# A third seven-product group per feed-forward chunk, weight sums made by adding DMAs, and banks handed on in two steps

## The chip, the cores and the metric

The kernel runs on one core of one Trainium2 chip. The metric is the device time of one execution, in microseconds. The kernel before took 2149.78 us, the median of three runs (2149.24 to 2150.08).

## The reference, cut to what matters

Two layers of a streaming encoder on 256 tokens with a model width of 2048, in float32. Layer 0 mixes tokens by sliding-window attention, layer 1 by a gated linear recurrence; both also attend into 256 memory tokens. Each layer ends in a feed-forward block of width 5632, and that block is all the change touches:

```python
        x = x + jnp.concatenate([mix, mem_out], axis=-1) @ w_o[i]
        gate, up = _split(rms_norm(x, norm_ffn[i]) @ w_gate_up[i], (D_FF, D_FF))
        x = x + (jax.nn.silu(gate) * up) @ w_down[i]
```

`w_gate_up` is 2048 by 11264 and `w_down` 5632 by 2048, for each of the two layers.

## The kernel before, in words

**Products in two parts.** TensorE works on float32r. Every weight block arrives by DMA in `raw`. ScalarE writes its rounded high part to `w_hi` (L644) and VectorE the remainder to `w_lo` (L1104), in the place of `raw`. The activations have a high and a low part too (`hT` for the normalised input, `gT` for the feed-forward's middle). A product is three matmuls of 128x128 by 128x512: high by high, low by high, high by low.

**Pieces and rings.** A piece is 256 rows by 512 columns of a weight (512 KB), two blocks of 128 rows. SyncE loads the pieces in the order in which they are used, into `raw`, a ring of eight. `w_hi` is a ring of four, so ScalarE can round piece n only once TensorE has used piece n-4 (`piece_used`). `pieces()` in the streams of ScalarE and VectorE is the frame of their order: step i first does the work written for step i, and then the split of piece i+3. Each engine runs its stream in order, so everything written for a step delays the splits behind it.

**The chunk loop.** The 5632 columns of gate and of up are cut into eleven chunks of 512. The first is computed plainly, the other ten in a loop of five passes over two halves, which are called passes here when counted one by one. One such pass has 16 pieces: for each of eight quads (256 rows of the weight) a piece of gate and a piece of up. A plain quad takes 24 matmuls (two row blocks, gate and up, two tiles of tokens, three parts). In two quads of a pass (`SEVEN = (2, 5)`) a Strassen-like scheme takes seven products in place of eight, so 21 matmuls. It needs three sums of the four weight blocks: `seven_sums` (VectorE, L1123, L1126, L1128) makes them one piece ahead of the group's split, `sums_high` (ScalarE) and `sums_low` (VectorE, L1134, L1135) split them. It also needs combinations of the activations, made once per layer (`seven_forms`).

**Banks.** Four PSUM banks belong to a pass (`own`), and the other four (`shared`) take the products that a seven-product group gives to several results. The next pass has these roles swapped. So the shared banks must be read out (`shared_products`, VectorE L1600 to L1605, with one copy by ScalarE) before the next pass begins, which `own_free` tells TensorE; the own banks are read right after the pass's last piece (`own_products`, L1613 to L1615).

**The product.** During pass n the result of pass n-1 is finished: tanh (ScalarE, step 2), `gate_silu` and `times_up` (VectorE, steps 4 and 5), a transpose in 32x32 squares to `turned`, sixteen DMAs of 32 KB that complete the transpose (SyncE's queue, put between the pieces 13, 14 and 15), and `moved_block` (VectorE L1209, step 12), which writes the low part of `gT`.

**Down.** After the loop `down_products` multiplies `gT` by `w_down`, with five seven-product groups of its own on each side. Before it starts, TensorE waits for `own_free` and for the twenty blocks of `gT` that the loop wrote.

## Time and profile before

| what | value |
|---|---|
| median of three runs | 2149.78 us |
| profiled execution, its own time | 2150.24 us |
| its span, first to last instruction | 2148.5 us |
| TensorE busy | 2135.4 us, 99% of the span |
| VectorE busy | 1682.8 us, 78% |
| ScalarE busy | 1119.4 us, 52% |
| GpSimd busy | 56.6 us, 3% |
| DMA: moved, mean rate | 435.56 MB, 203 GB/s |
| TensorE clock granted | 1.00 |

The busy time of an engine is a mean over stages that differ. The chain of waits is followed back from the last instruction, each step to what released it. In a timeline the instructions of an engine stand in order of time, with the idle time ahead of one in square brackets and the engine that ended it; like instructions that follow one another are one line with a count, and what is shown for them is the start of the first and the time to the end of the last. Two instructions of one engine overlap a little, so what a step costs is read from one start to the next.

### The profile page before, as it was taken

The page shows a single profiled execution, that of the slowest core. Times are in us where ns is not written, and L with a number is a line of the kernel's source. Part 1 is how long each engine was busy: PE and PEld are TensorE (multiplying, and loading weights), DVE is VectorE, ACT ScalarE, POOL GpSimd, SP SyncE. Part 2 cuts the span into 40 slices and gives each one's busy share as a digit, 9 for nine tenths or more (in the row PEclk, how much of TensorE's full clock was granted, in tenths as well). Part 3 has the DMA queues.
Part 4 walks back from the last instruction along what each step waited for, and adds up shares of the span by engine and source line. Part 5 has one row for each costly group of instructions (what it writes and reads, how often), then busy time and mean ns, then how long its engine had stood idle before and what let it go on. Part 6 is the DMA issues. An engine that isn't in the chain of part 4 may idle for free.

```text
span 2148.5 us, 29147 instructions
## 1 busy us (share of the span) xinstructions
PE 2135.4 (99%) x9992; PEld 1777.8 (83%) x9992; DVE 1682.8 (78%) x2139; ACT 1119.4 (52%) x1478; POOL 56.6 (3%) x99
## 2 busy tenths in 40 slices
PE   8999999999999999999999999999999999999999
PEld 7888888888888888888888888888888888888887
DVE  6657766898988898777666767667989898898775
ACT  7755654555455555454544544455554555555453
POOL 2101100000000000000000000000000000000000
PEclk9999999999999999999999999999999999999999
DMA  9765467667666766675665656577676667666664
GB/s 327 243 197 147 132 211 207 206 203 227 209 205 201 232 207 211 191 226 180 212 175 158 197 159 199 163 222 205 203 224 210 200 209 227 208 210 202 227 199 138
DMA packets 244568, 435.56 MB, mean 203 GB/s; under 512 B 23040, under 2 KB 43648, under 8 KB 244480
## 3 DMA queue, kind: packets, MB, share of 16 engines
q1 hardware_dynamic: 243392, 432.31, 65.1%
q10 hardware_dynamic: 1088, 2.10, 0.3%
q8 instruction: 52, 0.85, 0.2%
q14 instruction: 36, 0.29, 0.0%
HBM read 411.25 MB, written 2.10 MB: 192 GB/s over the span
## 4 chain that ended last, share of the span: by engine, by line
PE 99%; ACT 0%; DVE 0%; DMA 0%; issue 0%; DVEq 0%; SPq 0%; ACTq 0%
PE unit_bank L1886 30%; PE mix_bank L1928 24%; PE unit_bank L1928 24%; PE mix_bank L1898 7%; PE unit_bank L1898 7%; PE mix_bank L1886 4%; PE mix_bank L1979 1%; PE mix_bank L2109 1%; PE mix_bank L2044 0%; PE mix_bank L2006 0%; PE mix_bank L2053 0%; PE mix_bank L2095 0%; DVE w_lo L1104 0%; PE mix_bank L2017 0%; PE mix_bank L2028 0%; DMA source_T<-in_mem_T 0%
## 5 line engine op out<-in xcount | busy, mean ns | idle before, releaser
L644 ACT ACTIVATE w_hi<-raw 128x1024 fp32r<-128x1024 f32 x767 | 798.1, 1057 | 828.2 <-DVE sum_all L1128 166.5
L1104 DVE TENSOR_TENSOR w_lo<-raw,w_hi 128x1024 fp32r<-128x1024 f32 x767 | 923.4, 1221 | 353.0 <-ACT w_hi L644 346.8
L1886 PE MATMUL unit_bank<-w_hi,hT_hi 128*128 128x512 f32 (+1 forms) x576 | 181.2, 396 | 0.0
L1886 PE MATMUL unit_bank<-w_hi,hT_lo 128*128 128x512 f32 (+1 forms) x576 | 176.2, 387 | 0.0
L1886 PE MATMUL unit_bank<-w_lo,hT_hi 128*128 128x512 f32 (+1 forms) x576 | 175.9, 387 | 0.0
L1928 PE MATMUL unit_bank<-w_lo,hT_hi 128*128 128x512 f32 x480 | 147.9, 389 | 0.0
L1928 PE MATMUL mix_bank<-w_lo,hT_hi 128*128 128x512 f32 x480 | 147.8, 389 | 0.0
L1928 PE MATMUL mix_bank<-w_hi,hT_hi 128*128 128x512 f32 x480 | 147.8, 389 | 0.0
L1928 PE MATMUL unit_bank<-w_hi,hT_hi 128*128 128x512 f32 x480 | 147.8, 389 | 0.0
L1928 PE MATMUL unit_bank<-w_hi,hT_lo 128*128 128x512 f32 x480 | 147.8, 389 | 0.0
L1928 PE MATMUL mix_bank<-w_hi,hT_lo 128*128 128x512 f32 x480 | 147.7, 389 | 0.0
L1886 PEld LDWEIGHTS unit_bank<-w_hi,hT_lo 128*128 128x128 f32 x576 | 107.9, 188 | 21.7
L1886 PEld LDWEIGHTS unit_bank<-w_lo,hT_hi 128*128 128x128 f32 x576 | 107.9, 188 | 21.7
L1886 PEld LDWEIGHTS unit_bank<-w_hi,hT_hi 128*128 128x128 f32 x576 | 104.5, 188 | 18.2 <-DVE w_lo L1104 0.2
L1928 PEld LDWEIGHTS mix_bank<-w_hi,hT_hi 128*128 128x128 f32 x480 | 90.1, 188 | 18.7
L1928 PEld LDWEIGHTS unit_bank<-w_hi,hT_hi 128*128 128x128 f32 x480 | 90.1, 188 | 18.7
L1928 PEld LDWEIGHTS unit_bank<-w_lo,hT_hi 128*128 128x128 f32 x480 | 90.1, 188 | 18.7
L1928 PEld LDWEIGHTS mix_bank<-w_lo,hT_hi 128*128 128x128 f32 x480 | 90.1, 188 | 18.7
L1928 PEld LDWEIGHTS unit_bank<-w_hi,hT_lo 128*128 128x128 f32 x480 | 90.1, 188 | 18.7
L1928 PEld LDWEIGHTS mix_bank<-w_hi,hT_lo 128*128 128x128 f32 x480 | 90.1, 188 | 18.7
L1928 PE MATMUL mix_bank<-w_hi,gT_lo 128*128 128x512 f32 x272 | 83.8, 389 | 0.0
L1928 PE MATMUL unit_bank<-w_hi,gT_lo 128*128 128x512 f32 x272 | 83.8, 389 | 0.0
(427 smaller groups left out, 3602.7 us busy)
## 6 DMA issues: line engine op xcount, KB each, us to landing
raw<-in_w_gate_up SPq DMA_DIRECT2D x352, 512.0 KB, 4.4
raw<-in_w_down SPq DMA_DIRECT2D x176, 512.0 KB, 4.6
raw<-in_w_in_b SPq DMA_DIRECT2D x104, 512.0 KB, 3.7
raw<-in_w_o SPq DMA_DIRECT2D x64, 512.0 KB, 3.8
raw<-in_w_in_a SPq DMA_DIRECT2D x40, 512.0 KB, 3.7
moved<-turned SPq DMA_DIRECT2D x528, 32.0 KB, 2.5
raw<-in_w_mem_kv SPq DMA_DIRECT2D x31, 512.0 KB, 5.5
tanh_ff<-act_ff SPq DMA_DIRECT2D x112, 32.0 KB, 3.0
```

Source lines behind the costliest of these rows:

```text
L644: act.activation(w_hi[:, s, :, :], raw[:, r, :, :], ACT.Copy).then_inc(sems["hi_ready"], 1)
L1104: dve.tensor_tensor(w_lo[:, r, :, :], raw[:, r, :, :], w_hi[:, s, :, :].bitcast(F32), ALU.subtract).then_inc(sems["lo_ready"], 1)
L1886: ins = pe.matmul(all_banks[2 * pair + tile][:, 0:cols], stationary[part][:, kt + j, tile * P:(tile + 1) * P], b[:, j, 0:cols], start=open ...
L1898: ins = pe.matmul(bank[:, :], x_parts[part], w, start=start and m == 0, stop=stop and m == 2)
L1928: ins = pe.matmul(own[2 * tile + side][:, :], x[part][:, kt + j, tile * P:(tile + 1) * P], w, start=opens and j == 0 and m == 0, stop=clos ...
L1979: ins = pe.transpose(mix_bank[b][:, n * P:(n + 1) * P], src[:, n * width:(n + 1) * width], ident[:, :])
L2109: ins = pe.matmul(mix_bank[b][:, h * P:(h + 1) * P], early_key[:, h, :], whole(query_in, h * P + half, (4 * P - half, TILES), (size, block ...
```

## The change

What it does:

- **Groups.** `SEVEN` goes from (2, 5) to (2, 4, 6): three of the eight quads of a pass are seven-product groups. `QUAD_KTS` sets which weight rows a quad takes, so that the groups take rows at 4, 8 and 10 (before 4 and 10). The activations' combinations for the third come from `late_form` and `late_form_lo`, once per layer.
- **Sums.** Two of the three weight sums of a group are no longer computed by VectorE. SyncE loads the upper gate block twice, into both halves of a sum buffer (`spread`), and GpSimd's queue then issues two DMAs that add the lower gate block and the upper up block to it (`chunk_weight_sums`, `accum_op=ALU.add`). The gate piece of such a quad loads only its lower block. There are three such buffers; two of them lie where `kmT_b` and `vm_b` (layer 1's memory keys and values) lie, which are therefore written to the output's DRAM when layer 0's output projection begins, and read back during its down products. VectorE makes the other two sums (`third_sum`, `fourth_sum`), for which it now waits as late as the group's own split.
- **Banks.** The last group now ends at step 14 and not 12, so `shared_products` moves to step 14 (before 13) and `moved_block` to step 15 (before 12). The banks that the next pass's gate pieces write are released first (`own_free`), those of its up pieces second (`own_late`).
- **Silu** and its product with up move one step earlier (3 and 4); the transpose is now at step 6.
- **GpSimd.** The masks for the recurrence are made between the layers, since the third group's forms lie in their place.

```diff
-SEVEN = (2, 5)
-SEVEN_APART = 6
+SEVEN = (2, 4, 6)
+SEVEN_APART = 4
+QUAD_KTS = (0, 2, 4, 6, 8, 12, 10, 14)
+SPREAD_STEPS = (0, 1, 5)
+LAST_SEVEN = 2 * SEVEN[-1] + 2
...
+            def spread(w, kt, col, b, used):
+
+                sp.wait_ge(sems["piece_used"], t.value("piece_used", used))
+                for m in range(2):
+                    sp.dma_start(chunk_sums[b].two[:, m, :], w[kt * P:(kt + 1) * P, bass.ds(col, COLS)]).then_inc(sems[f"spread{b}"], 16)
...
+                spread_after = [2 * q + 2 - CHUNK_PIECES for q in SEVEN]
...
                     for half in range(2):
+                        col = j * (2 * COLS) + (1 + half) * COLS
                         for n in range(CHUNK_PIECES):
-                            piece(wg, n // 2 * 2, j * (2 * COLS) + (1 + half) * COLS + n % 2 * D_FF)
+                            load = lower_half_piece if n in SEVEN_PIECES else piece
+                            load(wg, QUAD_KTS[n // 2], col + n % 2 * D_FF)
+                            if n in SPREAD_STEPS:
+                                m = SPREAD_STEPS.index(n)
+                                spread(wg, QUAD_KTS[SEVEN[m]], col, chunk_sum(half, m), n + 1 - spread_after[m])
                             chunk_turns(n)
...
+            def chunk_weight_sums(layer):
...
+                            pool.wait_ge(sems[f"spread{b}"], t.next(f"spread{b}", 32))
+                            pool.dma_start(chunk_sums[b].two[:, 0, :], w[(kt + 1) * P:(kt + 2) * P, bass.ds(col, COLS)],
+                                           accum_op=ALU.add).then_inc(sems[f"summed{b}"], 16)
+                            pool.dma_start(chunk_sums[b].two[:, 1, :], w[kt * P:(kt + 1) * P, bass.ds(col + D_FF, COLS)],
+                                           accum_op=ALU.add).then_inc(sems[f"summed{b}"], 16)
...
+            def third_sum(sums, b):
+
+                r = slot[0] % RAW
+                blocks = four_blocks(raw, r)
+                dve.wait_ge(sems[f"summed{b}"], t.next(f"summed{b}", 32))
+                dve.wait_ge(sems[f"arrived{r}"], t.value(f"arrived{r}", -16))
+                dve.tensor_tensor(blocks[:, 0, :], sums.two[:, 1, :], blocks[:, 1, :], ALU.add).then_inc(sems["sum_ready"], 1)
+
+            def fourth_sum(sums, used):
...
+                dve.wait_ge(sems["piece_used"], t.value("at", used))
+                dve.wait_ge(sems[f"arrived{r + 1}"], t.value(f"arrived{r + 1}", -16))
+                dve.wait_ge(sems["sum_ready"], t.next("sum_ready"))
+                dve.tensor_tensor(sums.all[:, :], blocks[:, 0, :], blocks[:, 3, :], ALU.add).then_inc(sems["sum_ready"], 1)
+                dve.wait_ge(sems["sum_ready"], t.next("sum_ready"))
...
                 def shared_products(shared):
 
                     dve.wait_ge(sems["first_copied"], t.next("first_copied"))
-                    dve.wait_ge(sems["piece_used"], t.value("at", 1))
+                    dve.wait_ge(sems["piece_used"], t.value("at"))
                     dve.tensor_tensor(act_ff[:, 1, :], shared[3][:, :], up_ff[:, 0, :], ALU.subtract).then_inc(sems["dve_chain"], 1)
                     dve.wait_ge(sems["dve_chain"], t.next("dve_chain"))
-                    dve.tensor_tensor(act_ff[:, 0, :], shared[1][:, :], act_ff[:, 1, :], ALU.add)
-                    dve.tensor_tensor(up_ff[:, 1, :], shared[2][:, :], act_ff[:, 1, :], ALU.add).then_inc(sems["dve_chain"], 1)
+                    dve.tensor_tensor(up_ff[:, 1, :], shared[2][:, :], act_ff[:, 1, :], ALU.add).then_inc(sems["own_free"], 1)
+                    t.move("own_free")
+                    dve.tensor_tensor(act_ff[:, 0, :], shared[1][:, :], act_ff[:, 1, :], ALU.add).then_inc(sems["dve_chain"], 1)
...
-                def chunk(j, own, shared):
+                def chunk(j, half, own, shared):
 
                     for i in pieces(CHUNK_PIECES):
-                        if i + LEAD + 1 in SEVEN_PIECES:
-                            seven_sums(chunk_sums)
+                        if i + LEAD in SEVEN_PIECES:
+                            n = SEVEN_PIECES.index(i + LEAD)
+                            b = chunk_sum(half, n)
+                            third_sum(chunk_sums[b], b)
+                            fourth_sum(chunk_sums[b], i - (2 * SEVEN[n - 1] + 2) if n else 0)
                         if i + LEAD - 2 in SEVEN_PIECES:
-                            sums_low(chunk_sums)
+                            sums_low(chunk_sums[chunk_sum(half, SEVEN_PIECES.index(i + LEAD - 2))])
+                        if i == 3:
+                            gate_silu()
                         if i == 4:
-                            gate_silu()
-                        if i == 5:
                             times_up()
-                        if i == 12:
+                        if i == 6:
+                            turn_product()
+                        if i == LAST_SEVEN:
+                            shared_products(shared)
+                        if i == LAST_SEVEN + 1:
                             moved_block(gT, j * 4, "gT_ready")
-                        if i == 13:
-                            shared_products(shared)
                     own_products(own)
```

VectorE's stream around the end of a pass. `w_lo` is the split of a piece, `act_ff` and `up_ff` read the banks (shared ones first, the pass's own after), `gT_lo` is `moved_block`. Before:

```order
L1104 TENSOR_TENSOR w_lo<-raw,w_hi 128x1024 [waits hi_ready]
...
L1209 TENSOR_TENSOR gT_lo<-moved,gT_hi 128x4x4x32
...
L1104 TENSOR_TENSOR w_lo<-raw,w_hi 128x1024 [waits hi_ready]
L1600 TENSOR_TENSOR act_ff<-mix_bank,up_ff 128x512 [waits piece_used,first_copied]
...
L1602 TENSOR_TENSOR act_ff<-mix_bank,act_ff 128x512 [waits dve_chain]
L1603 TENSOR_TENSOR up_ff<-mix_bank,act_ff 128x512
...
L1605 TENSOR_TENSOR act_ff<-mix_bank,up_ff 128x512 [waits dve_chain]
...
L1104 TENSOR_TENSOR w_lo<-raw,w_hi 128x1024 [waits hi_ready]
...
L1613 TENSOR_TENSOR act_ff<-unit_bank,act_ff 128x512 [waits own_free]
```

The same place in the changed kernel:

```order
L1172 TENSOR_TENSOR w_lo<-raw,w_hi 128x1024 [waits hi_ready]
L1688 TENSOR_TENSOR act_ff<-mix_bank,up_ff 128x512 [waits piece_used,first_copied]
...
L1690 TENSOR_TENSOR up_ff<-mix_bank,act_ff 128x512 [waits dve_chain]
L1692 TENSOR_TENSOR act_ff<-mix_bank,act_ff 128x512
...
L1695 TENSOR_TENSOR act_ff<-mix_bank,up_ff 128x512 [waits dve_chain]
...
L1172 TENSOR_TENSOR w_lo<-raw,w_hi 128x1024 [waits hi_ready]
...
L1295 TENSOR_TENSOR gT_lo<-moved,gT_hi 128x4x4x32
...
L1172 TENSOR_TENSOR w_lo<-raw,w_hi 128x1024 [waits hi_ready]
L1703 TENSOR_TENSOR act_ff<-unit_bank,act_ff 128x512 [waits own_late,piece_used]
```

The shared banks' four sums stand one step nearer to the end (three splits lay between them and the own banks' sums, now two), and the two `gT_lo` have moved from ahead of them to behind them.

VectorE's stream between the first and the second group of a pass, from silu on. `raw<-` is a sum that is written back to the ring, `turned` the transpose. Before:

```order
L1581 SCALAR_TENSOR_TENSOR tanh_ff<-tanh_ff,act_ff 128x512 [waits tanh_ff_ready]
...
L1104 TENSOR_TENSOR w_lo<-raw,w_hi 128x1024 [waits hi_ready]
...
L1589 SCALAR_TENSOR_TENSOR up_ff<-up_ff,half_rs_87,tanh_ff 128x512 [waits shared_free]
...
L1185 STREAM_TRANSPOSE turned<-up_ff 128x4x4x32 [waits dve_chain]
...
L1104 TENSOR_TENSOR w_lo<-raw,w_hi 128x1024 [waits hi_ready]
...
L1123 TENSOR_TENSOR sums<-raw 128x1024 [waits arrived3,arrived2]
```

And in the changed kernel:

```order
L1667 SCALAR_TENSOR_TENSOR tanh_ff<-tanh_ff,act_ff 128x512 [waits tanh_ff_ready]
...
L1172 TENSOR_TENSOR w_lo<-raw,w_hi 128x1024 [waits hi_ready]
...
L1675 SCALAR_TENSOR_TENSOR up_ff<-up_ff,half_rs_94,tanh_ff 128x512 [waits shared_free]
...
L1172 TENSOR_TENSOR w_lo<-raw,w_hi 128x1024 [waits hi_ready]
L1204 REGISTER_ALU [waits summed1]
L1205 TENSOR_TENSOR raw<-key_sums_69,raw 128x512 [waits arrived0]
L1213 REGISTER_ALU [waits arrived1,piece_used]
L1214 TENSOR_TENSOR sum_all<-raw 128x512 [waits sum_ready]
...
L1172 TENSOR_TENSOR w_lo<-raw,w_hi 128x1024 [waits hi_ready]
...
L1271 STREAM_TRANSPOSE turned<-up_ff 128x4x4x32 [waits dve_chain]
```

The second group begins two pieces earlier in the pass than before, so its two sums and its splits now stand in the stretch that holds silu, the product with up and the transpose.

## Rows read from the trace of the kernel before

**Rows 1.** The page, part 4: shares of the chain that ended last.
```profile
PE 99%; ACT 0%; DVE 0%; DMA 0%; issue 0%; DVEq 0%; SPq 0%; ACTq 0%
```

**Rows 2.** Windows: window, busy us by engine (instructions), granted clock, DMA share, GB/s.
```profile
372.19:793.79 421.60, 421.60 (x1861) 349.12 (x1861) 373.87 (x420) 218.43 (x250) 0.00 (x0) 1.00 0.68 211
16.00:24.00 8.00, 8.00 (x37) 6.61 (x36) 6.84 (x12) 5.81 (x11) 0.00 (x0) 1.00 1.05 408
```

**Rows 3.** Timeline, TensorE: start us, us, line, what, count; two starts in one pass.
```profile
467.23 0.39 PE L1898 MATMUL unit_bank<-w_hi,hT_hi 128*128 128x512 f32 x1
...
487.63 0.62 PE L1928 MATMUL unit_bank<-w_hi,hT_hi 128*128 128x512 f32 x2
```

**Rows 4.** Timeline, VectorE, first half of that pass; idle time before in brackets.
```profile
456.63 1.29 DVE L1613 TENSOR_TENSOR act_ff<-mix_bank,act_ff 128x512 f32<-128x512 f32 x2
...
459.04 1.21 DVE L1123 TENSOR_TENSOR sums<-raw 128x1024 f32<-128x1024 f32 x1
460.29 0.69 DVE L1126 TENSOR_TENSOR raw<-sums,raw 128x512 f32<-128x512 f32 x1
461.01 0.69 DVE L1128 TENSOR_TENSOR sum_all<-raw 128x512 f32<-128x512 f32 x1
...
465.09 1.23 DVE L1104 TENSOR_TENSOR w_lo<-raw,w_hi 128x1024 fp32r<-128x1024 f32 x1 [0.95 <-ACT w_hi L644]
466.55 1.23 DVE L1134 TENSOR_TENSOR sums_lo<-sums,sums_hi 128x1024 fp32r<-128x1024 f32 x1 [0.24 <-ACT sums_hi L658]
...
468.30 1.22 DVE L1104 TENSOR_TENSOR w_lo<-raw,w_hi 128x1024 fp32r<-128x1024 f32 x1
469.43 1.28 DVE L1581 SCALAR_TENSOR_TENSOR tanh_ff<-tanh_ff,act_ff 128x512 f32<-128x512 f32 x2
470.63 1.22 DVE L1104 TENSOR_TENSOR w_lo<-raw,w_hi 128x1024 fp32r<-128x1024 f32 x1
471.77 1.41 DVE L1589 SCALAR_TENSOR_TENSOR up_ff<-up_ff,half_rs,tanh_ff 128x512 f32<-128x512 f32 x2
473.21 1.30 DVE L1185 STREAM_TRANSPOSE turned<-up_ff 128x512 f32<-128x512 f32 x2
474.44 1.18 DVE L1104 TENSOR_TENSOR w_lo<-raw,w_hi 128x1024 fp32r<-128x1024 f32 x1
```

**Rows 5.** Timeline, VectorE, end of the same pass.
```profile
488.92 1.23 DVE L1104 TENSOR_TENSOR w_lo<-raw,w_hi 128x1024 fp32r<-128x1024 f32 x1 [2.99 <-ACT w_hi L644]
490.06 1.29 DVE L1209 TENSOR_TENSOR gT_lo<-moved,gT_hi 128x512 f32 x2
491.39 1.23 DVE L1104 TENSOR_TENSOR w_lo<-raw,w_hi 128x1024 fp32r<-128x1024 f32 x1
492.53 0.69 DVE L1600 TENSOR_TENSOR act_ff<-mix_bank,up_ff 128x512 f32<-128x512 f32 x1
...
495.19 3.49 DVE L1104 TENSOR_TENSOR w_lo<-raw,w_hi 128x1024 fp32r<-128x1024 f32 x3
```

**Rows 6.** Timeline, ScalarE, same pass.
```profile
461.82 1.06 ACT L644 ACTIVATE w_hi<-raw 128x1024 fp32r<-128x1024 f32 x1 [4.21 <-DVE sum_all L1128]
462.78 1.32 ACT L939 ACTIVATE tanh_ff<-act_ff,half_rs 128x512 f32<-128x512 f32 x2
```

**Rows 7.** Timeline, SyncE's queue, same pass.
```profile
474.55 3.69 SPq L432 DMA_DIRECT2D moved<-turned  x6
...
485.96 15.97 SPq L417 DMA_DIRECT2D raw<-in_w_gate_up  x9
```

**Rows 8.** DMA issues: transfer, count, KB each, median us to landing.
```profile
raw<-in_w_gate_up SPq DMA_DIRECT2D x352, 512.0 KB, 4.4
...
x_tok<-in_mem SPq DMA_DIRECT2D x4, 512.0 KB, 10.9
...
raw<-in_w_mem_kv SPq DMA_DIRECT2D x2, 256.0 KB, 3.8
```

More of the change, by code:

```diff
@@ L278, in trunk @@
         assert rest + 2 * 2 * 3 * P * 4 <= nc.sbuf_usable_end
-        chunk_sums = Sums(sums, sums_lo, sum_all, sum_all_lo, sums_hi)
+        chunk_sums = tuple(Sums(two, two_lo, sum_all, sum_all_lo, sums_hi)
+                           for two, two_lo in ((sums, sums_lo), key_sums[0], key_sums[1]))
+        chunk_forms = [tuple(f[:, g, :, :] for f in forms) for g in range(2)]
+        chunk_forms.append(tuple(f[:, :, :] for f in late_forms))
         over = arena + 2 * FT * SEQ * 4
@@ L498, in projection_ffn @@
                 wo = w_o[layer, :, :]
+                if layer == 0:
+                    for n, tile in enumerate((kmT_b, vm_b)):
+                        sp.dma_start(aside(n), tile[:, :, :].rearrange("p a n -> p (a n)")).then_inc(sems["parked"], 16)
                 for kts in MIXED_KTS:
@@ L526, in projection_ffn @@
                         moves(down_turns[p])(n)
+                        if layer == 0 and p == 0 and n == 10:
+                            for m, tile in enumerate((kmT_b, vm_b)):
+                                sp.dma_start(tile[:, :, :].rearrange("p a n -> p (a n)"), aside(m)).then_inc(sems["restored"], 16)
             wa = w_in_a[0, :, :]
@@ L968, in projection_ffn @@
                     for half, (own, shared) in enumerate(chunk_banks):
-                        chunk(j * 2 + half, shared)
+                        chunk(j * 2 + half, half, shared)
                 def store(c):
@@ L1677, in projection_ffn @@
                     for half, (own, shared) in enumerate(chunk_banks):
-                        chunk(j * 2 + half, own, shared)
+                        chunk(j * 2 + half, half, own, shared)
                 def down_form(n):
@@ L1899, in product, with seven_products @@
                 return ins
-            def seven_products(x, kt, forms, n, sums, own, shared, first, last, shared_ready):
+            def seven_products(x, kt, forms, sums, own, shared, first, last, shared_ready):
                 s, r = slot[0] % RING, slot[0] % RAW
@@ L1945, in down_products @@
                         pe.wait_ge(sems["gT_ready"], t.next("gT_ready", TILES))
+                    if p == 0 and (q, side) == (0, 1):
+                        pe.wait_ge(sems["own_late"], t.next("own_late"))
                     if q not in DOWN_SEVEN:
@@ L1960, in chunk_products @@
                         n = SEVEN.index(q)
-                        seven_products(hT, 2 * q, forms, n, chunk_sums, own, shared, n == 0, n == len(SEVEN) - 1, evicted)
+                        seven_products(hT, QUAD_KTS[q], chunk_forms[n], chunk_sums[chunk_sum(half, n)], own, shared, n == 0, n == len(SEVEN) - 1, evicted)
                         continue
                     for side in range(2):
-                        plain_piece(hT, 2 * q, side, own, q == 0, q == CHUNK_PIECES // 2 - 1)
+                        if q == 0 and side == 1:
+                            pe.wait_ge(sems["own_late"], t.next("own_late"))
+                        plain_piece(hT, QUAD_KTS[q], side, own, q == 0, q == CHUNK_PIECES // 2 - 1)
             def unit(stationary, pair, kts=ALL_KTS, opens=True, closes=True, cols=COLS):
```

146 lines of the change are left out of this document (105 added, 41 removed).

## The prediction

> **What bounds the kernel now.** I read the page's chain first: TensorE makes up 99% of it [rows 1]. Then the windows, cut to the ten passes of layer 0's chunk loop: they take 421.60 us and TensorE is busy in all of it, at a granted clock of 1.00 [rows 2]. So a pass takes 42.16 us. By the code it holds six plain quads and two groups, 6 x 24 + 2 x 21 = 186 matmuls; 42.16 / 186 = 0.2267 us for one, 2.72 us for a plain piece (12) and 4.76 us for a group (21). No pass waits for anything. What matters next is how near the other engines are to being late, since a matmul taken away brings everybody's deadline nearer. VectorE is busy for 373.87 of the 421.60 us [rows 2], 37.4 us a pass; DMA engines 0.68 of the time at 211 GB/s. Last I followed one pass in the timelines, to see where VectorE stands when a group begins. The first group of the pass begins at 467.23 [rows 3] and needs the split of its second piece, which starts on VectorE at 465.09 [rows 4] and takes 1.23 us: ready at 466.32, 0.91 us early. That is all the slack there is. Later in the pass VectorE waits for TensorE (2.99 us idle ahead of 488.92) [rows 5].
>
> **The matmuls removed.** One more group in each of 20 passes: 20 x 3 x 0.2267 = 13.6 us less, a pass of 183 matmuls or 41.48 us.
>
> **VectorE, in sum.** The two wide sums of a pass go (459.04, 1.21 us each); the third group adds two sums of 0.69 us and its low parts, 1.75 us (466.55 to 468.30) [rows 4]. That is 37.4 - 2.4 + 3.1 = 38.1 us in 41.48, 92%. It fits in the mean, so the mean doesn't decide; the order does.
>
> **VectorE, from the last group to the next pass's first.** The order in which its work now stands is this. Count from T, the moment TensorE goes on after the pass's last group; in the trace of before the like moment (after its second group) is 487.63 [rows 3]. Splits go no further ahead, because `w_hi` has four places: the third-next split can start only when the group has ended. ScalarE's and VectorE's first split follow, VectorE's at 488.92, so T + 1.29 [rows 5]. From there, start to start:
>
> - the split of the next pass's piece 0, 1.14 us (488.92 to 490.06) [rows 5]: T + 2.43
> - four sums from the shared banks, 2.66 us (492.53 to 495.19) [rows 5]: T + 5.09
> - split of piece 1: T + 6.23
> - two `gT_lo`; their 1.33 us (490.06 to 491.39) [rows 5] hold a short wait, and two instructions of that size take 1.20 (469.43 to 470.63) [rows 4], so 1.20: T + 7.43
> - split of piece 2: T + 8.57
> - four sums from the own banks, 2.41 us (456.63 to 459.04) [rows 4]: T + 10.98
> - split of piece 3: T + 12.12, where `third_sum` starts; it ends 0.69 later, T + 12.81
> - ScalarE had waited for this sum; then it rounds piece 4, makes the two tanh, and rounds piece 5. In before, the same chain leads from the end of the last sum (461.01 + 0.69 = 461.70) by ScalarE at 461.82 and 462.78 [rows 6] to VectorE's split at 465.09 [rows 4]: 3.39 us. So the split starts at T + 16.20 and ends at T + 17.43.
>
> TensorE has six plain pieces for that time, 6 x 2.72 = 16.32 us. It waits 1.11 us at the first group. In before the shared sums and `gT_lo` lie before the end of the pass, and VectorE begins the own sums 0.3 us after it (456.63, for a pass that starts four plain pieces ahead of 467.23, at 456.35) [rows 3, 4].
>
> **VectorE, on to the second group.** It has no pause in which to catch up: low parts start 1.46 us after that split (465.09 to 466.55) and take 1.75, silu 1.20, a split 1.14, the product with up 1.33 (471.77 to 473.21 is 1.44 with the wait ahead of the transpose), a split 1.14 [rows 4]: T + 24.22. Then the third sum (0.69 and 0.03 of semaphore, as 460.29 to 461.01 shows) and the fourth, 0.72 each. ScalarE rounds piece 8 once the third sum is there: 0.12 to start (461.70 to 461.82) and 1.06 [rows 6], so VectorE's split starts at T + 26.11, the transposes take 1.23 (473.21 to 474.44) and the split of piece 9 ends at T + 29.70. TensorE: group started at T + 17.43, 4.76, two plain pieces 5.44: T + 27.63. It waits 2.07 us. Before, this stretch held no second group: it comes two pieces later there. For the third group the count goes on: low parts 1.75, two splits 2.28, two sums 1.4 (the fourth also waits for the second group's end, T + 34.46), two splits 2.3: T + 37.7 for a need at T + 39.90, no wait.
>
> A pass then takes 41.48 + 1.11 + 2.07 = 44.66 us, 2.50 more than before, with VectorE idle at its end again; so the lag doesn't grow from pass to pass. Of the ten passes of a layer the first has no shared sums and no `gT_lo` ahead of it: its first group is ready at 9.1 us for a need at 10.88, its second 0.33 us late.
>
> **Into the down products.** TensorE waits there for all twenty blocks of `gT`. The last two are now written at T + 6.23 to T + 7.5, and TensorE gets there at T + 5.44: 2.1 us, each layer. Before they were written some 8 us ahead (490.06 for a pass that ends at 498.5) [rows 5].
>
> **The sum.** 18 passes x (1.11 + 2.07) = 57.2; two first passes x 0.33 = 0.7; two down starts 4.2; less 13.6: +48.5 us. On the profiled execution's 2150.24 us (span 2148.5 and 1.7 around it) that makes 2198.7; the median of the runs is 0.5 lower, so 2198.3.
>
> **The adding DMAs.** No row shows one. Bytes: 12 transfers of 0.26 MB a pass come and three halves of pieces go, +2.4 MB; 211 GB/s x 42.16 us is 8.9 MB, so 11.3 MB in 44.66 us, 252 GB/s, or 287 if an add counts its bytes twice, since it reads its target too. An early window moves 408 GB/s for 8 us [rows 2]. Only if the six adds (1.6 MB) held the engines for over five times their bytes would the rings be full. Time: SyncE is held by `turned`, now ready at T - 16.1 (the transposes end at T + 28.5 and the next T comes 44.66 later, with 0.1 for the wait); its sixteen small DMAs with the loads between take 11.4 us (474.55 to 485.96) [rows 7], so the next pass's piece 0 is issued at T - 4.6 and its first spread about T - 4.2. The sum is wanted at T + 12.1: 16.3 us for a spread and an add. At 3.8 us each, as the 256 KB loads [rows 8], that is 7.6; at 10.9 each, as the 512 KB loads of the crowded start [rows 8], it is 21.8, 5.5 us late in each pass, some +105 us. I take the first, it is nearer in size; both ends go into the range. Piece 0 itself has 4.8 us for a landing of 4.4 in the median [rows 8]; each us that it is late costs one in a pass, 18 in all. Less than nothing it can't cost: what VectorE saves by it is already out of the list. The Trainium skill (DMA: Bandwidth & Descriptors, "Where 436 GB/s comes from") gives about 358 GB/s as the limit of HBM for a core; the trace's 408 is above it, and at 358 the 12.8 MB would still take 36 us of 44.66, hidden.
>
> GpSimd issues the adds with nothing else to do: it is not busy at all in this window [rows 2]. The Trainium skill (SBUF — State Buffer, "Who interferes with whom") says that descriptor generation on GpSimd starves while VectorE runs in a two-port mode, but that tensor_tensor has none; by that the adds are not held, and no run here shows it.
>
> **At nothing:** the forms (once a layer, under the plain chunk), the masks (GpSimd is free between the layers), moving 1 MB aside and back (waited for a whole stage later). Together at most a few us.
>
> **The rivals.**
> - *The lag is absorbed*, the other side of no change: 13.6 us less, and the 4.2 at the down starts at most: 2136 to 2140. It needs 3.2 us less on VectorE between T and the second group. For it speaks the mean (38.1 of 41.48); against it, every term is a row of this same loop and the slack of 0.91 us in before leaves no room.
> - *The waits are half of what I count*, 0.7 us a pass: 18 x 0.7 + 5 - 13.6 = +4 us, within or near no change, 2150 to 2160.
> - *The DMAs decide*: adds or piece 0 late by 1 to 5.5 us a pass, 2216 to 2300. For it: a burst of eight transfers that start within 4 us after SyncE was held; against it: 408 GB/s in the early window.
>
> **How the numbers follow.** Forecast 0.68, with its own range 2182 to 2215 (0.5 us a pass to either side, and a few more for DMAs). Absorbed 0.07, halved waits 0.07, DMAs 0.18, of which half stays under 2250. The range 2176 to 2250 leaves out about 0.2. A measurement of this kernel can't tell less than 0.2% (4.3 us) from no change. Faster 0.08, same 0.04, slower 0.88.
>
> **What would show it.** Right: passes of about 44.7 us; TensorE idle about 1.1 us ahead of a pass's first group and 2.1 ahead of the second, ended by VectorE's `w_lo`, none ahead of the third; 2 us at each down start, ended by `gT_lo`; VectorE without a pause from the last group on to the second. Wrong: passes of 41.5 us; waits ended by a DMA into `raw` or by the sum's semaphore; VectorE idle before `third_sum`; instructions of VectorE longer than in before beside the adds.

## The result, and the profile after

| kernel | median of its runs | range | runs | ratio to before, 95% interval |
|---|---|---|---|---|
| before | 2149.88 us | 2149.24 to 2150.08 | 4 | |
| changed | 2216.63 us | 2215.01 to 2219.17 | 4 | 1.0312, 1.0294 to 1.0330 |

The change costs 66.8 us where I forecast 48.5. The direction and the place were right, the size was 18 us short. (The kernel before has one run more here than in the table ahead of the prediction.)

The profiled execution took 2217.19 us, its span is 2214.9, and its mean granted clock 0.994 (before 1.000). The chain of the page, which was TensorE for 99% [rows 1]:

```profile
PE 73%; DVE 8%; DMA 7%; issue 5%; ACT 4%; SPq 2%; DVEq 0%; ACTq 0%
```

It now runs over VectorE, SyncE's queue and transfers too: TensorE waits. The list of its waits says for whom (line, what it waited for, us in all, times, longest):

```profile
PE mix_bank L2023 <- DVE w_lo L1172: 27.6, 20, 1.8
PE unit_bank L2023 <- DVE w_lo L1172: 22.4, 16, 1.8
...
PE unit_bank L2053 <- issue: 4.1, 2, 2.1
```

That is 36 waits at the start of a seven-product group (L2023): two in each of the 18 passes that are not the first of a layer. They end with VectorE's split. The last line is the start of the down products, once per layer. The windows answer to [rows 2]: the ten passes of layer 0, and one typical pass.

```profile
372.80:825.60 452.80, 425.46 (x1831) 345.21 (x1830) 377.93 (x440) 233.56 (x271) 48.98 (x56) 0.99 0.81 246
517.89:562.74 44.85, 42.12 (x184) 34.20 (x184) 37.88 (x44) 23.24 (x28) 5.25 (x6) 1.00 0.81 246
```

VectorE's work per pass hardly grew (37.8 against 37.4 us); the pass grew from 42.16 to 44.85. Where the time goes, TensorE's timeline of that pass shows at the starts of its three groups and of the next pass's first:

```profile
517.89 0.50 PE L2023 MATMUL mix_bank<-w_hi,hT_hi 128*128 128x512 f32 x1 [0.95 <-DVE w_lo L1172]
...
530.19 0.50 PE L2023 MATMUL mix_bank<-w_hi,hT_hi 128*128 128x512 f32 x1 [1.78 <-DVE w_lo L1172]
...
540.54 0.39 PE L2023 MATMUL mix_bank<-w_hi,hT_hi 128*128 128x512 f32 x1
...
562.74 0.50 PE L2023 MATMUL unit_bank<-w_hi,hT_hi 128*128 128x512 f32 x1 [0.95 <-DVE w_lo L1172]
```

The third group comes 10.35 us after the second, which is one group and two plain pieces (10.20) and 0.15: no wait, as forecast. From the first to the second it is 12.30, against the same 10.20: 2.1 us lost. From the third to the next pass's first it is 22.20, where one group and six plain pieces take 21.08: 1.1 us lost. The idle time in brackets is some 0.16 us smaller than the wait, since the end of a matmul's row overlaps the next. The first matmul after a wait stands as 0.50 instead of 0.39 us, and the next starts 0.34 us later instead of 0.227.

VectorE after the same moment T = 545.31 (the third group's start and its 4.77), to be held against [rows 4, 5]:

```profile
546.60 1.23 DVE L1172 TENSOR_TENSOR w_lo<-raw,w_hi 128x1024 fp32r<-128x1024 f32 x1 [2.88 <-ACT w_hi L705]
547.74 0.68 DVE L1688 TENSOR_TENSOR act_ff<-unit_bank,up_ff 128x512 f32<-128x512 f32 x1
...
553.86 1.28 DVE L1703 TENSOR_TENSOR act_ff<-mix_bank,act_ff 128x512 f32<-128x512 f32 x2
...
557.39 0.68 DVE L1205 TENSOR_TENSOR raw<-sums,raw 128x512 f32<-128x512 f32 x1
558.84 0.69 DVE L1214 TENSOR_TENSOR sum_all<-raw 128x512 f32<-128x512 f32 x1 [0.77 <-DMA raw<-in_w_gate_up]
559.66 1.23 DVE L1172 TENSOR_TENSOR w_lo<-raw,w_hi 128x1024 fp32r<-128x1024 f32 x1
561.46 1.23 DVE L1172 TENSOR_TENSOR w_lo<-raw,w_hi 128x1024 fp32r<-128x1024 f32 x1 [0.57 <-ACT w_hi L705]
...
572.57 1.30 DVE L1271 STREAM_TRANSPOSE turned<-up_ff 128x512 f32<-128x512 f32 x2
573.79 1.18 DVE L1172 TENSOR_TENSOR w_lo<-raw,w_hi 128x1024 fp32r<-128x1024 f32 x1
```

Reading it from T: the first split at T + 1.29 (forecast 1.29), own sums at 8.55 (8.57), third sum at 12.08 (12.12), the split that the first group needs at 16.15 (16.20), the one that the second needs ends at 574.97, T + 29.66 (29.70). The count from rows of before holds to 0.05 us over thirty instructions. One thing in it was not forecast: the fourth sum waits 0.77 us for the load of piece 5, which was issued late (T + 1.0) and landed 12.3 us after its issue. In this pass it costs nothing, since ScalarE's chain ends at the same time: VectorE's next split but one still waits 0.57 us for ScalarE.

**The part that was missing: the clock.** In some passes the matmuls after the second wait run slower. TensorE's timeline of one such pass, and the windows of that stretch and of the one behind it (the last three figures are granted clock, DMA share, GB/s):

```profile
438.93 0.50 PE L2023 MATMUL mix_bank<-w_hi,hT_hi 128*128 128x512 f32 x1 [1.78 <-DVE w_lo L1172]
...
440.43 0.62 PE L2023 MATMUL unit_bank<-w_hi,hT_hi 128*128 128x512 f32 x1
440.84 0.63 PE L2023 MATMUL unit_bank<-w_hi,hT_lo 128*128 128x512 f32 x1
...
443.83 0.40 PE L2023 MATMUL unit_bank<-key_sums_lo,forms_hi 128*128 128x512 f32 x1
```

```profile
440.43:443.83 3.40, 3.40 (x9) 2.64 (x8) 3.06 (x4) 0.00 (x0) 0.00 (x0) 0.50 0.31 71
443.83:447.00 3.17, 3.17 (x15) 2.64 (x14) 0.81 (x2) 1.37 (x2) 0.00 (x0) 1.00 0.54 185
```

From 440.43 to 443.83 eight matmuls start 0.42 to 0.43 us apart instead of 0.227, at a granted clock of 0.50 (the level of 1.2 GHz), 1.5 us after the wait is over, and then it is 1.00 again. The loss is 8 x 0.2 = 1.6 us. The Trainium skill (TensorE: Matmul & The Clock Gate, "Wait — 56ns, not 53.3ns?") gives 426.7 ns between such matmuls at the lower clock; the trace agrees with 426 to 427 inside such a stretch. This happens in 6 of the 18 passes with waits (from 440.4, 621.3, 757.9 and from 1590.7, 1727.2, 1908.2) and at both down starts. The down start of layer 0:

```profile
825.57 0.71 PE L2053 MATMUL unit_bank<-w_hi,gT_hi 128*128 128x512 f32 x2 [2.01 <-issue]
826.11 1.03 PE L2053 MATMUL unit_bank<-w_hi,gT_lo 128*128 128x512 f32 x2
826.94 1.05 PE L2053 MATMUL unit_bank<-w_lo,gT_hi 128*128 128x512 f32 x2
```

Pairs come 0.83 to 0.85 us apart instead of 0.453. The releaser of that wait is not named, but VectorE's `gT_lo` ends at 825.47 (824.18, 1.29 us for its two), 0.10 us before.

**The account**, from starts of the profiled executions: the loop of layer 0 with its down start went from 421.6 to 452.9 us, that of layer 1 from 421.6 to 452.6, each down phase takes 1.7 more, the start of the kernel 0.6: 31.3 + 31.0 + 3.4 + 0.6 = 66.3, which is what the span grew by (66.4; another 0.6 of the execution lies outside the span). In my terms:

| term | forecast | measured |
|---|---|---|
| 60 matmuls less | -13.6 | -13.6 |
| 18 passes with two waits, each | 3.18, in all 57.2 | 44.85 - 41.48 = 3.37, in all 60.7 |
| first passes | 0.7 | about 1.0 |
| waits at the two down starts (start to start) | 4.2 | 2.17 + 2.23 = 4.4 |
| slower matmuls at the lowered clock | 0 | 6 x 1.6 + 2 x 1.7 = 13.0 |
| the kernel's start, one longer wait (1.39 instead of 0.95) | 0 | 1.0 |
| sum | +48.5 | +66.5 |

(The 1.7 at a down start holds 0.1 for starting again. The longer wait is the one at 744.13: the fourth sum ahead of it waited 0.91 us for its piece, so in that pass a transfer did cost TensorE 0.4 us.)

**The queues.** SyncE's and GpSimd's timelines around T:

```profile
540.88 0.38 SPq L431 DMA_DIRECT2D raw<-in_w_gate_up  x1
541.51 0.82 SPq L448 DMA_DIRECT2D sums<-in_w_gate_up  x2
```

```profile
547.01 0.87 POOL L637 DMA_DIRECT2D sums<-in_w_gate_up  x1 [27.90 <-DMA sums<-in_w_gate_up]
547.74 1.02 POOL L639 DMA_DIRECT2D sums<-in_w_gate_up  x1
...
557.02 0.87 POOL L639 DMA_DIRECT2D key_sums<-in_w_gate_up  x1 [6.17 <-issue]
```

Piece 0 is issued at T - 4.4 (forecast T - 4.6) and the first spread at T - 3.8. The spread takes 5.5 us (541.51 to the first add at 547.01), and both adds are issued by T + 3.5, for a need at T + 12.1. Between the rows shown stands a third add, at 549.97; the fourth is issued only after 6.17 us for which the profile names no releaser; it still is in time. The landings say more: the second add landed at 556.66, 0.35 us before the fourth was issued. All 39 such pauses of over 0.4 us in the changed kernel's trace (those with no releaser named) end 0.25 to 0.35 us after the landing of the add two places before. Landings got slower everywhere in the loop, a piece from 4.4 us [rows 8] to 6.5 in the median:

```profile
raw<-in_w_gate_up SPq DMA_DIRECT2D x292, 512.0 KB, 6.5
...
key_sums<-in_w_gate_up SPq DMA_DIRECT2D x80, 256.0 KB, 6.6
key_sums<-in_w_gate_up POOLq DMA_DIRECT2D x80, 256.0 KB, 6.8
```

### The profile page after: what moved, and what is told of

It is laid out like the page before. It is cut to its first block, busy times and chain, and to the rows that moved or that the text cites. A ratio compares the mean times of both kernels' runs of the same rounds, so it can differ in the third digit from the quotient of the medians.

```text
span 2214.9 us, 30087 instructions
## 1 busy us (share of the span) xinstructions
PE 2146.5 (97%) x9932; PEld 1772.1 (80%) x9932; DVE 1697.4 (77%) x2193; ACT 1149.8 (52%) x1522; POOL 162.8 (7%) x220
## 4 chain that ended last, share of the span: by engine, by line
PE 73%; DVE 8%; DMA 7%; issue 5%; ACT 4%; SPq 2%; DVEq 0%; ACTq 0%
PE unit_bank L2011 29%; PE mix_bank L2053 12%; PE unit_bank L2053 12%; DMA raw<-in_w_gate_up 7%; PE unit_bank L2023 6%; PE mix_bank L2023 6%; PE mix_bank L2011 4%; DVE w_lo L1172 3%; ACT w_hi L705 2%; SPq L462 1%; DVE turned L1271 1%; PE mix_bank L2108 1%; PE mix_bank L2238 1%; DVE raw L1205 1%; DVE tanh_ff L1667 1%
## 5 line engine op out<-in xcount | busy, mean ns | idle before, releaser
L2011 PEld LDWEIGHTS unit_bank<-w_lo,hT_hi 128*128 128x128 f32 x576 | 107.9, 188 | 21.7
L2011 PEld LDWEIGHTS unit_bank<-w_hi,hT_lo 128*128 128x128 f32 x576 | 107.9, 188 | 21.7
L2053 PE MATMUL mix_bank<-w_hi,hT_hi 128*128 128x512 f32 x400 | 123.1, 389 | 0.0
L2053 PE MATMUL unit_bank<-w_hi,hT_lo 128*128 128x512 f32 x400 | 123.1, 389 | 0.0
L2053 PE MATMUL unit_bank<-w_hi,hT_hi 128*128 128x512 f32 x400 | 123.1, 389 | 0.0
L2053 PE MATMUL mix_bank<-w_hi,hT_lo 128*128 128x512 f32 x400 | 123.1, 389 | 0.0
L2053 PE MATMUL mix_bank<-w_lo,hT_hi 128*128 128x512 f32 x400 | 123.1, 389 | 0.0
L2053 PE MATMUL unit_bank<-w_lo,hT_hi 128*128 128x512 f32 x400 | 123.1, 389 | 0.0
L2011 PEld LDWEIGHTS unit_bank<-w_hi,hT_hi 128*128 128x128 f32 x576 | 104.4, 188 | 18.2 <-DVE w_lo L1172 0.2
L2053 PE MATMUL unit_bank<-w_hi,gT_hi 128*128 128x512 f32 x272 | 84.8, 394 | 4.1 <-issue 4.1
L2053 PEld LDWEIGHTS unit_bank<-w_lo,hT_hi 128*128 128x128 f32 x400 | 75.1, 188 | 15.6
L2053 PEld LDWEIGHTS unit_bank<-w_hi,hT_hi 128*128 128x128 f32 x400 | 75.1, 188 | 15.6
L2053 PEld LDWEIGHTS unit_bank<-w_hi,hT_lo 128*128 128x128 f32 x400 | 75.1, 188 | 15.6
```

The costliest lines, as they stand in the source:

```text
L2011: ins = pe.matmul(all_banks[2 * pair + tile][:, 0:cols], stationary[part][:, kt + j, tile * P:(tile + 1) * P], b[:, j, 0:cols], start=open ...
L2053: ins = pe.matmul(own[2 * tile + side][:, :], x[part][:, kt + j, tile * P:(tile + 1) * P], w, start=opens and j == 0 and m == 0, stop=clos ...
```

## The experiments

Theory 1: VectorE's work in order, from the last group of a pass to the second of the next, decides; 13 of the 67 us are the lowered clock behind the waits that it makes. Rivals: the transfers decide and VectorE only shows it; VectorE has room and something else is slow. Each run is compared with runs of the kernel before on the same chip. Two further variants with less work for VectorE (`gT_lo` on a quarter of its columns, alone and with the lighter silu and a later tanh) have no result.

### Loads in place of adds

```diff
-pool.dma_start(chunk_sums[b].two[:, 0, :], w[(kt + 1) * P:(kt + 2) * P, bass.ds(col, COLS)], accum_op=ALU.add)
+pool.dma_start(chunk_sums[b].two[:, 0, :], w[(kt + 1) * P:(kt + 2) * P, bass.ds(col, COLS)])
```

(and the second add likewise)

> The 120 adding DMAs become plain loads of the same bytes into the same buffers from the same queue, so the weight sums are not sums; all else stands. Theory (VectorE's work between a pass's last group and the next pass's second group is 3.2 us longer than TensorE's): no change from 2216.6, 2211 to 2218 (at most the 0.8 us that the fourth sum waits for a piece goes, which is covered by ScalarE). Rival 1 (adding in flight is slow and holds the rings): at least 10 us faster, 2150 to 2205.

Measured: 2216.64 us (2215.14 to 2218.47), ratio 1.0309 (1.0292 to 1.0326), TensorE's waits as in the changed kernel (the other banks' line is 22.0 us in 16):

```profile
PE mix_bank L2021 <- DVE w_lo L1170: 28.5, 20, 1.8
```

So that a transfer adds costs nothing here. It does show in the queue: in this run four such transfers are issued from 544.74 to 549.46, with no pause but the wait for the second spread, where the adds stopped after three.

### Two groups, with all the rest of the change

```diff
-SEVEN = (2, 4, 6)
+SEVEN = (2, 5)
...
-SPREAD_STEPS = (0, 1, 5)
+SPREAD_STEPS = (0, 3)
```

> One part alone: two groups as before the change, at quads 2 and 5, with the rest of the change (sums by adding DMAs, two sums by VectorE at the group's own step, banks in two steps, silu a step earlier). VectorE does 2.4 us less in a pass than before and the second group lies later. Theory: no wait, the same 186 matmuls, so the time before: 2150 (2147 to 2153). Rival 1 or 2 (the new DMAs cost by themselves): 2156 or more.

Measured: 2150.08 us (2149.51 to 2151.04), ratio 1.0002 (0.9992 to 1.0011), no wait in any pass. The window of layer 0's loop, to compare with [rows 2]:

```profile
372.50:794.00 421.50, 421.50 (x1862) 349.00 (x1861) 350.28 (x401) 219.05 (x251) 31.59 (x36) 1.00 0.80 246
```

VectorE is 23.6 us less busy than before and the time is the same: TensorE has the whole of it either way. With two groups the adding DMAs (two thirds of their number), the handover and the parked key buffers cost nothing; the whole loss comes with the third group and what it does to the order.

### Tanh and silu one step later

```diff
-if i == 2:
+if i == 3:
     gate_tanh()      # ScalarE
...
-if i == 3:
+if i == 4:
     gate_silu()      # VectorE
-if i == 4:
+if i == 5:
     times_up()
```

> Only order: ScalarE's two tanh one step later (3, before 2), VectorE's silu and its product with up one step later (4 and 5). The tanh no longer lie between ScalarE's splits of the first group's two pieces, behind which VectorE stood idle, and the fourth sum's idle time goes too. Theory: first wait 1.1 to about 0.2 us, second 2.0 to about 1.4, some 27 us in 18 passes, and the lowered clock after the longer waits comes more rarely: 2185 (2178 to 2194). Rivals 1 and 2: within 5 us of 2216.6.

Measured: 2189.39 us (2186.05 to 2191.83), ratio 1.0181 (1.0164 to 1.0198). ScalarE's two tanh leave the chain that leads to the first group. The first wait is gone or under 0.9 us, the second is 1.2 to 1.7 us still, once 2.5:

```profile
PE mix_bank L2023 <- DVE w_lo L1172: 18.3, 13, 2.5
PE unit_bank L2023 <- DVE w_lo L1172: 15.1, 16, 1.7
```

27 us less for one line on each of two engines. A transfer-bound loop would not have moved.

### The product's low part before the last group's end

```diff
-if i == LAST_SEVEN + 1:
+if i == LAST_SEVEN - 1:
     moved_block(gT, j * 4, "gT_ready")
```

(on both engines; two small buffers change places so that nothing is overwritten too early)

> Against the changed kernel: gT's block is written at step 13 (before 15), while VectorE waits for the third group's end; for that the sums' high parts and the forms change places in memory. 1.2 us leave VectorE's stretch, and the down products find gT ready. Theory: the stretch is shorter by 1.2, but the fourth sum then waits for its piece, which lands 13.4 us after the third group's end in the changed kernel's trace, so the first wait falls by 0.8 (1.1 to 0.3), the second stays; at each down start 2.1 of wait and 1.9 of lowered clock go: 18 x 0.8 + 2 x 4 = 22, so 2195 (2188 to 2204). Rival 2 (the DMAs' bytes set the pace): only the down starts' 8 us, 2208 or more.

Measured: 2195.74 us (2194.55 to 2197.97), ratio 1.0214 (1.0198 to 1.0229). No wait at the down starts, and the group waits fall by 6.5 us in sum:

```profile
PE mix_bank L2022 <- DVE w_lo L1171: 23.5, 18, 1.8
PE unit_bank L2022 <- DVE w_lo L1171: 20.0, 14, 1.9
```

The second wait is 1.80 us still, as in the changed kernel, but only three passes have slower matmuls after it instead of six. The gain of 20.9 us is the down starts with their slower matmuls (4.4 + 3.4), 6.5 of waits, three stretches at the lower clock (4.8) and some restarts. So the expected time came true, but not by its terms: 14.4 us were expected from the waits, and no fewer slow stretches in the passes. VectorE's 1.2 us less bring the first wait down by 0.4 us in the mean and not by 0.8, since loads come late behind them. In a pass of layer 0, for example, ScalarE waits 1.42, 1.85 and 2.28 us for loads into `raw` (680.73, 683.64 and 686.98), VectorE's split at 684.73 waits 0.88 for ScalarE, and the fourth sum at 691.02 waits 0.93 for its piece. The loads are a second limit, close behind VectorE's order.

### Silu and its product with up on 64 of 512 columns

```diff
-gate_silu()
+small_silu()     # tanh_ff[:, s, 0:64]
-times_up()
+small_up()       # up_ff[:, s, 0:64]
```

> The changed kernel with silu and its product with up in the ten passes of a layer's loop computed on 64 of 512 columns; the rest of those columns is left out, so the two instructions of each pair shrink from 0.6 us to some 0.1 us. Nothing else is touched. Theory 1 (VectorE's order sets the waits, and the lowered clock after them is part of their price): about 2 us of VectorE's work go between a pass's first and second group, so the wait of 1.95 us ahead of the second group goes (18 x 1.95 = 35 us), and with it the six stretches of slower matmuls in the passes (6 x 1.6 = 9.6 us): 2216.6 - 45 = 2172, range 2166 to 2178. The wait of 1.1 us ahead of the first group and that of 2 us at each down start stay as they are. Theory 2 (the transfers set the pace, VectorE only shows it): 2205 or more, with the second wait still there and ended by a transfer. Theory 3 (the lowered clock has to do with something other than the waits): the waits go and the clock cost stays, 2181.

Measured: 2172.32 us (2170.75 to 2175.01), ratio 1.0107 (1.0090 to 1.0124). The first wait and the down starts stay (0.95 each in the trace), the second is gone, and none of the passes has slower matmuls; the one stretch of them that is left in the trace is at a down start. The other down start has none behind a wait as long as in the changed kernel (2.01).

```profile
PE mix_bank L2040 <- DVE w_lo L1173: 9.5, 10, 1.0
PE unit_bank L2040 <- DVE w_lo L1173: 8.3, 8, 1.3
...
PE unit_bank L2070 <- issue: 4.5, 2, 2.5
```

Its gain over the changed kernel is 44.3 us; 18 x 1.95 for the waits and 9.5 for the clock make 44.6. So the slow stretches in the passes go with the second waits; waits of 0.95 have none behind them. Transfers were the same in number and size, even at 259 GB/s instead of 246, so they did not set the loop's time.

### One handover of the shared banks

```diff
 pe.wait_ge(sems["own_free"], t.next("own_free"))
+pe.wait_ge(sems["own_late"], t.next("own_late"))
 for q in range(CHUNK_PIECES // 2):
...
-        if q == 0 and side == 1:
-            pe.wait_ge(sems["own_late"], t.next("own_late"))
```

> The changed kernel, but TensorE waits at the start of a pass for both releases of the shared banks at once, as the kernel before did, and not in two steps. Theory 1: no difference, 2216.6 within 3 us: the fourth shared sum ends about 5.1 us after the last group by my count and TensorE begins the next pass at 5.44, so even the later release is there in time. Theory 2 (the two steps save a wait that the trace hides): the next pass starts some tenths of a us late in each of 18 passes, 2220 to 2230.

Measured: 2216.31 us (2214.11 to 2216.74), ratio 1.0304 (1.0287 to 1.0321). No difference. In the changed kernel's trace the fourth shared sum ends at 550.47, T + 5.16, and the next pass starts at T + 5.44: with one handover there is still 0.3 us to spare, so the two steps save nothing.

### The kernel before, with one sum computed twice

```diff
-def seven_sums(sums):
+def seven_sums(sums, again=False):
...
+    if again:   # in the first group of each pass
+        dve.tensor_tensor(sums.two[:, :, :], blocks[:, 1:3, :], blocks[:, 0:1, :].broadcast_to([P, 2, COLS]), ALU.add).then_inc(sems["dve_chain"], 1)
+        dve.wait_ge(sems["dve_chain"], t.next("dve_chain"))
     dve.tensor_tensor(sums.two[:, :, :], blocks[:, 1:3, :], blocks[:, 0:1, :].broadcast_to([P, 2, COLS]),
...
```

> The kernel before, with the wide sum of the first group of each pass computed twice in a row on VectorE (1.21 us and 0.04 for its semaphore more in each of 20 passes; the result is the same). Theory 1 (the slack ahead of a pass's first group is 0.91 us and is all there is): the split that the group waits for comes 1.25 - 0.91 = 0.34 us late, and with 0.1 to 0.2 us to start again 0.45 to 0.55 us a pass: 2158 to 2161, or from 2156 if the restart costs nothing. Theory 2 (VectorE is busy for 89% of the loop and has 4.6 us to spare in a pass, so 1.25 more hides): 2149.9, no difference.

Measured: 2162.97 us (2162.43 to 2163.39), ratio 1.0059 (1.0042 to 1.0075): 12.9 us or 0.65 a pass, where I gave it 0.45 to 0.55 (2158 to 2161). VectorE, then TensorE at the first group:

```profile
467.93 1.23 DVE L1104 TENSOR_TENSOR w_lo<-raw,w_hi 128x1024 fp32r<-128x1024 f32 x1 [0.95 <-ACT w_hi L644]
```

```profile
468.36 0.61 PE L1931 MATMUL unit_bank<-w_lo,hT_hi 128*128 128x512 f32 x2
469.21 0.50 PE L1901 MATMUL unit_bank<-w_hi,hT_hi 128*128 128x512 f32 x1 [0.24 <-DVE w_lo L1104]
469.55 0.40 PE L1901 MATMUL unit_bank<-w_hi,hT_lo 128*128 128x512 f32 x1
```

The pair at 468.36 would have been followed at 468.81; the split ends at 469.16 and the group starts at 469.21. So 0.35 us late by the count (1.25 against a slack of 0.91), 0.05 for the semaphore, 0.11 for the slower first matmul and some hundredths in each of the next few; the rest of the 0.65 is about 0.1 further on. Being late at all costs about 0.3 us on top of the lateness. Behind waits as short as this (0.24 us shown) no matmul of the loops ran at the lower clock (1.000). The slack of 0.91 is thus real and is all there was: VectorE's 89% of busy time gave no room.

### Spreads and moves later

```diff
-SPREAD_STEPS = (0, 1, 5)
+SPREAD_STEPS = (0, 5, 8)
-chunk_turns = moves({13: (0, 6), 14: (6, 12), 15: (12, 16)})
+chunk_turns = moves({15: (0, 16)})
```

(together with the edits above on tanh and silu and on the product's low part)

> As the run with all, but the transpose stays at step 6 and SyncE issues all sixteen small DMAs, now together behind the last load of the pass. Theory: no or little wait at the first group, 0.5 to 1.2 us at the second, partly from the next pass's piece 0 that SyncE issues late: 2158 (2150 to 2168). Rival 2: above 2175, as in the run with the later tanh alone less the 8 us at the down starts.

Measured: 2164.67 us (2163.34 to 2166.23), ratio 1.0067 (1.0052 to 1.0083). The first wait is gone, the second is 0.7 to 1.7 us, once 2.7 (the transpose still stands ahead of the split of piece 9); TensorE's waits for `w_lo` are 11.5 us in 10 and 9.9 in 10. So this order keeps the first deadline and misses the second.

### All of it: an order that keeps every deadline

The kernel above with two edits more: the transpose goes behind the split of piece 9, and SyncE's moves stand at the pieces 13 to 15 again, but only eight of the sixteen. GpSimd's queue takes the others (behind one small load into `ang`).

```diff
-if i == 6:
+if i == 7:
     turn_product()
-chunk_turns = moves({15: (0, 16)})
+chunk_turns = moves({13: (0, 3), 14: (3, 6), 15: (6, 8)})
...
+for m in range(8, 16):     # on GpSimd's queue
+    a, b = m // QUADS, m % QUADS
+    pool.dma_start(moved[0][b * QUAD:(b + 1) * QUAD, a, :, :, :],
+                   turned[0][a * QUAD:(a + 1) * QUAD, b, :, :, :]).then_inc(sems["moved_sw"], 16)
```

> Three groups and five changes of order: tanh at step 3, silu 4, product with up 5, transpose at step 7 behind the second group's last split, gT's block at step 13, the spreads at load steps 0, 5 and 8 (before 0, 1, 5), and half of the sixteen small transposing DMAs on GpSimd's queue, so that SyncE comes earlier to the next pass's loads. By the rows of the changed kernel VectorE is then in time at both groups. Theory: passes of 41.5 to 41.8 us, 2149.9 - 13.6 = 2136, up to 2145. Rival 2 (bytes): passes stay above 42.5 with VectorE or ScalarE waiting for pieces, 2160 or more.

Measured: **2137.25 us** (2136.95 to 2138.40), ratio to before 0.9943 (0.9929 to 0.9956). It beats both kernels: 12.7 us under before, of the 13.6 that the removed matmuls are worth. One pass, from a first group to the next:

```profile
424.83:466.35 41.52, 41.52 (x185) 34.28 (x184) 37.53 (x45) 22.91 (x28) 8.92 (x14) 1.00 0.90 269
```

41.5 us (41.9 in two passes of the twenty), TensorE busy in all of it at a granted clock of 1.00, with VectorE as busy as before (37.5 us). VectorE around the second group of a pass:

```profile
515.67 2.36 DVE L1186 TENSOR_TENSOR w_lo<-raw,w_hi 128x1024 fp32r<-128x1024 f32 x2
517.95 1.30 DVE L1285 STREAM_TRANSPOSE turned<-up_ff 128x512 f32<-128x512 f32 x2
```

The two splits end at 518.03, and the group starts at 508.21 + 10.20 = 518.41: 0.38 us early, and the transpose follows instead of leading.

### The same with all moves on SyncE's queue

```diff
-chunk_turns = moves({13: (0, 3), 14: (3, 6), 15: (6, 8)})
+chunk_turns = moves({13: (0, 6), 14: (6, 12), 15: (12, 16)})
```

(and the eight moves go from GpSimd's queue)

> The improved kernel (2137.25 us) with all sixteen moves of the product on SyncE's queue again, at steps 13, 14 and 15, and nothing on GpSimd's queue but the adds. The transpose stays at step 7, behind the split of piece 9. Theory 1 (SyncE's queue is the second thing that can be late): in that kernel the transpose ends about 2 us later than in the changed one, sixteen moves hold SyncE for some 11 us, and piece 0 of the next pass is issued about 2 us ahead of its use where it lands 4 to 6 us after issue: 2 to 4 us late in each of 18 passes, 2180 to 2215, with TensorE's wait ahead of the first matmuls of a pass, ended by VectorE's or ScalarE's part of a piece that waited for its load. Theory 2 (the order on VectorE is all that matters): 2137, as with half of the moves on GpSimd's queue.

Measured: 2188.99 us (2187.16 to 2189.51), ratio 1.0181 (1.0164 to 1.0198): 52 us more than the kernel above, with the same order on VectorE. Piece 0 is issued at 450.52, 2.1 us ahead of the end of the last group (452.60); there it is 442.74 for 450.03, 7.3 us ahead. The lateness does not show where I expected it, at the start of a pass; it shows as ScalarE and VectorE waiting for transfers inside the pass (ScalarE 1.25, 1.29 and 0.50 us for the pieces 0 to 2), and so at the groups. VectorE's third sum:

```profile
465.79 0.69 DVE L1204 TENSOR_TENSOR raw<-sums,raw 128x512 f32<-128x512 f32 x1 [0.71 <-DMA sums<-in_w_gate_up]
```

TensorE's waits for VectorE's `w_lo` at group starts are 27.1 us in 34 here, and a pass takes 43.7 us in layer 0's mean (437.2 us for ten) instead of 41.6. SyncE's queue is the second deadline, mostly hidden in the changed kernel by VectorE's: the later a transpose, the later sixteen DMAs of about 0.6 us each in front of the next pass's loads.

## Why the forecast was right in kind and short in size

- **What bounds the kernel** and **the matmuls removed**: right. The improved order shows the worth of the removed matmuls, 12.7 of 13.6 us, and the twice computed sum shows the slack of 0.91 us.
- **VectorE, from the last group to the first, and on to the second**: right, to 0.05 us at T + 12.1, T + 16.2 and T + 29.7. The waits are 1.12 and 1.95 in place of 1.11 and 2.07: VectorE's part is exact, and the second wait is shorter by what TensorE lost in starting again after the first (0.16).
- **No wait at the third group**: right. **Into the down products**: 2.2 and 2.2 us for 2.1.
- **The adding DMAs**: right that they are hidden. SyncE was held to T - 4.4 for a forecast of T - 4.6, and the sums were there in time. The landing of 12.3 us for piece 5 stood above the upper bound that I had kept for the range (10.9), and it was harmless in most passes only since ScalarE's chain ended at the same moment. In the kernel with the low part moved such loads take half of the gain at the first group, and with all moves on SyncE's queue late loads cost time in every pass. (5.5 us in each of 18 passes are 99 us and not the 105 that I wrote; nothing rests on it.)
- **The sum**: here it fell short. The step was "18 passes x (1.11 + 2.07) = 57.2", "two down starts 4.2": I took the lateness as the whole price of a wait. The measured price has two more parts. Starting again costs 0.2 us per pass net of what the second wait absorbs (3.4 us in 18 passes), and stretches of eight matmuls at the lower clock cost 13.0 us. The loop of before has no wait from which to read either. But its trace showed the lower clock: from 8.97 to 13.24 us, at the kernel's start, ten matmuls come 0.427 us apart. I had not priced a start from rest by them. Nor was the range right by its own reasons: the 2182 to 2215 that I gave to this mechanism ends 1.6 us below the measured time, and only the share kept for late DMAs carried the stated range to 2250.
- **The lag is absorbed**: false for this order. It is true for the improved one, whose split for the second group ends at T + 26.1 (518.03, with T = 491.89) and not at T + 29.7: 3.5 us less, as the rival's condition said ("3.2 us less").
- **The DMAs decide**: false, by the kernel without adds and by the one with the lighter silu. My range for this rival began at 2216, and the time came out at its edge for another reason: a match in time is not a match in mechanism.
- **The waits are half**: false.

## What to carry over

When an engine's stream is a fixed order, add up what stands in it between two deadlines, from rows of the same loop, and compare each sum with the bounding engine's time for that stretch; the mean share of busy time (92% by the forecast) says nothing of it. To each new stop of TensorE add about 0.3 us for starting again, and, where the stops are near 2 us, allow for matmuls at half the clock behind some of them. If a deadline is missed, first try another order, and follow the queue that waits for the piece you moved: here the new order (tanh, silu and its product, the transpose, `gT`'s low part and the spreads) was worth 79 us together with fewer moves on SyncE's queue, and 28 without that.

## What the runs showed that I had not expected

- **The clock falls after some stops and not after others of the same length.** After waits of 1.76 to 1.81 us shown, six passes of 18 have eight matmuls 0.43 us apart and twelve have none. It isn't tied to a pass: in the kernel with plain loads the stretches begin at 529.5, 621.7, 802.6 and 1591.1, 1772.0, 1952.9. With the product's low part moved there are three, with tanh later one. What picks them is open. Six stretches more or less are 9.6 us, and the runs of the changed kernel spread by 4.2 us where those of before spread by 0.84.
- **Adding DMAs hold GpSimd's queue.** After three of 256 KB the next was issued 6.17 us after the queue was free, just behind the landing of the second of them, as in all 39 such pauses; yet the third was issued with two still on their way, so no plain limit on adds in flight explains it. The queue's instruction for an add took 0.85 to 1.21 us; plain loads of the same shape took 0.55 us each with few exceptions and had no such pause, beside the same stream on VectorE. The pauses go with the adds, then, and not with VectorE's work. The Trainium skill (SBUF — State Buffer, "Who interferes with whom") lets VectorE hold up this queue's descriptors only in a two-port mode, which tensor_tensor hasn't; the traces agree.
- **The traffic was far from a limit that mattered.** A pass of the improved kernel moves 269 GB/s at a DMA share of 0.90 with TensorE never idle.
